# A Hyena/MLA encoder layer: the inverse DFT of its spectral stages as three products of f16 parts, three bins behind

## What is computed

```
def fft_conv(z, kf, bias):
    L = z.shape[1]
    zf32 = z.astype(jnp.float32)
    zf = jnp.fft.rfft(zf32, n=2 * L, axis=1)
    y = jnp.fft.irfft(zf * kf, n=2 * L, axis=1)[:, :L]
    return y + zf32 * bias.astype(jnp.float32)

def hyena_mixer(u, ...):
    v, x1, x2 = jnp.split(short_conv(u, conv_w, conv_b), 3, axis=-1)
    kf = hyena_filters(L, ...)                 # spectra of the implicit filters
    z = x1 * fft_conv(v, kf[:, 0], bias[0])
    z = x2 * fft_conv(z, kf[:, 1], bias[1])
```

## Time and profile before

| | us |
|---|---|
| median of 3 runs | 2887.83 (2886.19 to 2893.82) |
| the profiled execution | 2882.89 |
| its span in the profile | 2881.0 |

### The profile page before, as it was taken

One profiled execution on the slowest core, in us unless ns is written; L12 is line 12 of the kernel. 1 busy time (PEld: TensorE's weight loads), 2 busy tenths in 40 slices (PEclk: granted clock), 3 DMA queues, 4 the chain that ended last, 5 costly groups with the idle time before them and its releaser, 6 DMA issues. The chain is left out here.

```text
span 2881.0 us, 47562 instructions
## 1 busy us (share of the span) xinstructions
PE 2532.7 (88%) x17257; PEld 1429.3 (50%) x17257; DVE 2024.9 (70%) x2938; ACT 1772.1 (62%) x2980; POOL 1107.0 (38%) x1048
## 2 busy tenths in 40 slices
PE   6899999959999999988897896999910999999997
PEld 4455555525555555553332232455510666676664
DVE  5456555548888888878897896544367777777773
ACT  6644444329999999988555654433240777766761
POOL 1221212138888888877106600122120233333331
PEclk9999999959999999999999998999955999999998
DMA  7423323325311111107786787445341677776752
GB/s 183 125 59 92 92 80 90 98 64 181 106 24 24 38 38 38 38 16 251 270 302 221 276 302 261 135 151 165 110 166 34 203 234 224 226 221 211 221 150 57
DMA packets 269184, 416.04 MB, mean 144 GB/s; under 512 B 55646, under 2 KB 149214, under 8 KB 267424
## 3 DMA queue, kind: packets, MB, share of 16 engines
q1 hardware_dynamic: 219952, 344.39, 37.6%
q0 software_dynamic: 10752, 37.75, 5.4%
q10 hardware_dynamic: 38288, 31.37, 3.8%
HBM read 280.56 MB, written 132.86 MB: 143 GB/s over the span
## 5 line engine op out<-in xcount | busy, mean ns | idle before, releaser
L1162 POOL TENSOR_TENSOR at_p<-at_pf,at_p 128x512 f16<-128x512 f32 x424 | 510.6, 1214 | 138.0 <-ACT at_p L1296 110.7
L1424 DVE TENSOR_REDUCE at_mxs<-at_pM 128x1 f32<-128x512 f32 x512 | 342.4, 685 | 74.1 <-PE at_pM L1323 62.6
L1295 ACT ACTIVATE at_pf<-at_pS,at_scale 128x512 f32<-128x512 f32 x520 | 358.3, 689 | 30.1 <-PE at_pS L1348 29.2
L1296 ACT ACTIVATE at_p<-at_pS,at_scale 128x512 f16<-128x512 f32 x520 | 355.3, 683 | 0.0
L1367 PEld LDWEIGHTS at_pO<-at_vv,at_p 128*128 128x128 f16 x4160 | 233.8, 97 | 140.7 <-POOL at_p L1162 31.8
L1367 PE MATMUL at_pO<-at_vv,at_p 128*128 128x129 f16 x4160 | 267.8, 207 | 8.3 <-POOL at_p L1162 6.5
L1323 PE MATMUL at_pM<-at_k,at_q 96*128 96x512 f16 x512 | 190.2, 390 | 27.6 <-DVE at_q L1410 17.2
L1346 PE MATMUL at_pS<-at_q,at_k 97*128 97x512 f16 (+1 forms) x528 | 200.2, 379 | 3.9 <-issue 2.2
L1347 PE MATMUL at_pS<-at_q,at_k 96*128 96x512 f16 (+1 forms) x528 | 199.8, 378 | 0.0
L1348 PE MATMUL at_pS<-at_q,at_k 96*128 96x512 f16 (+1 forms) x528 | 198.6, 376 | 0.0
L2405 PE MATMUL mg_pU<-z,mg_yT 128*128 128x512 f16 x576 | 171.6, 380 | 2.8 <-DVE z L2493 2.1
(11 more groups left out here) (400 smaller groups left out, 6097.6 us busy)
## 6 DMA issues: line engine op xcount, KB each, us to landing
sp_rows<-s_F SPq DMA_DIRECT2D x76, 512.0 KB, 5.4
s_F<-fs_a SPq DMA_DIRECT2D x72, 512.0 KB, 3.0
mo_raw<-in_w_gate SPq DMA_DIRECT2D x32, 1024.0 KB
mo_raw<-in_w_up SPq DMA_DIRECT2D x32, 1024.0 KB, 6.9
mo_down<-in_w_down SPq DMA_DIRECT2D x32, 1024.0 KB, 4.9
s_G<-sp_gg SPq DMA_DIRECT2D x72, 256.0 KB, 4.1
sp_tab<-tab_spec SPq DMA_DIRECT2D x76, 224.0 KB, 3.9
s_QK<-pj_R ACTq DMA_DIRECT2D x18, 768.0 KB, 4.7
```

What stands on the lines that cost most here:

```text
L1162: eng.tensor_tensor(p2[r][:, :], pf[:, r, :], p1[r][:, :], ALU.subtract).then_inc(own_done if n in own else others_done, 1)
L1295: act.activation(pf[:, n % 4, :], pS[n % 2][:, 0:QB], ACT.Exp, scale=scale[:, 0:1])
L1296: act.activation(p1[n % 4][:, :], pS[n % 2][:, 0:QB], ACT.Exp, scale=scale[:, 0:1]).then_inc(pS_free, 1)
L1424: dve.tensor_reduce(mxs[:, j // NC, j % NC:j % NC + 1], pM[j % 2][:, :], AX.X, ALU.max).then_inc(pM_free, 1)
```

## The change

The inverse tables become pairs of f16 parts like the forward ones (same bytes). The product of the spectra, still made in f32 by VectorE, is split into an f16 high part by ScalarE (`split_pk`, after `move_x` of the next step) and an f16 low part by GpSimd, which subtracts the high part from the product. The inverse DFT is then six f16 products (high x high, low table x high, high table x low, two halves each) in place of two f32 ones, and it runs three steps behind instead of two. `pk` has two buffers (RING), its parts have four (LAG + 1); the output buffers become three, and a result is stored six steps behind instead of seven. The product is scaled down by 2^-18 so that it fits f16, which the last scale takes back.

```diff
--- before.py
+++ after.py
@@ -76,7 +76,7 @@
         back[b, :, P:] = np.concatenate([of_im, -of_re], 0)[:, order]
         spec[b, :, P:] = folded_spectrum(L, b)
     return (first.reshape(2, P, P).transpose(1, 0, 2), last.reshape(2, P, P).transpose(1, 0, 2),
-            np.concatenate([back.astype(np.float32), in_halves(spec)], -1))
+            np.concatenate([in_halves(back), in_halves(spec)], -1))
 
 
 TAB_SCALE = 2.0 ** 10
@@ -1887,8 +1887,10 @@
     N0 = NB[0] + 1
     STEPS = N0 + NB[1] + 1
     H = N2
-    PREP, LAG = 2, 2
-    ROWS, SPLIT, TABS, OUTS, STORE_LAG = 4, 3, 6, 4, 7
+    PREP, LAG = 2, 3
+    ROWS, SPLIT, TABS, OUTS, STORE_LAG = 4, 3, 6, 3, 6
+    RING, PK_SCALE = 2, 2.0 ** -18
+    assert 8 * MOST ** 2 * PK_SCALE <= MOST
     TW = P + N2
     with ExitStack() as ctx:
         def sb(name, shape, dt=F32):
@@ -1902,13 +1904,16 @@
 
         tab = [sb(f"tab{r}", [P, 2 * P + TW]) for r in range(TABS)]
         tabs = [t[:, 2 * P:].bitcast(F16) for t in tab]
+        backs = [t[:, 0:2 * P].bitcast(F16) for t in tab]
+        back_hi, back_lo = ([t[:, at:at + 2 * P] for t in backs] for at in (0, 2 * P))
         tab_hi, tab_lo = ([t[:, at:at + TW] for t in tabs] for at in (0, TW))
         cross = sb("cross", [P, P])
         cross_hi = cross[:, :].bitcast(F16)[:, 0:P]
         rows_in = [sb(f"rows{r}", [P, 2, DH]) for r in range(ROWS)]
         high, low = ([sb(f"{n}{r}", [P, 2, DH], F16) for r in range(SPLIT)] for n in ("high", "low"))
         xs = sb("xs", [P, 2, DH])
-        pk = [sb(f"pk{r}", [P, 2, DH]) for r in range(LAG + 1)]
+        pk = [sb(f"pk{r}", [P, 2, DH]) for r in range(RING)]
+        pk_hi, pk_lo = ([sb(f"pk_{n}{r}", [P, 2, DH], F16) for r in range(LAG + 1)] for n in ("hi", "lo"))
         gg, inverse = sb("gg", [P, OUTS, DH]), sb("inverse", [P, 2, DH])
         total, each, scale, back = sb("total", [P, 2]), sb("each", [P, NT + 4]), sb("scale", [P, 2]), sb("back", [P, 2])
         sized_by, mhalf = sb("sized_by", [P, 2]), sb("mhalf", [P, 1])
@@ -1923,6 +1928,7 @@
         cross_in, high_made, low_made = sem("cross_in"), sem("high_made"), sem("low_made")
         x_made, x_moved, k_made, multiplied = sem("x_made"), sem("x_moved"), sem("k_made"), sem("multiplied")
         g_made, g_moved, unscaled = sem("g_made"), sem("g_moved"), sem("unscaled")
+        pk_high, pk_low = sem("pk_high"), sem("pk_low")
         g_out = [sem(f"g_out{r}") for r in range(OUTS)]
         src, dst = ([stage_rows(io[x], g) for g in range(2)] for x in ("F", "G"))
         block = ctx.enter_context(nc.Block())
@@ -1970,9 +1976,19 @@
             pool.wait_ge(consts, 1)
             pool.wait_ge(floored, 1)
             pool.tensor_tensor(scale[:, 0:1], sized_by[:, 0:1], mhalf[:, :], ALU.pow).then_inc(rooted, 1)
+            for n in range(STEPS):
+                r = n % (LAG + 1)
+                pool.wait_ge(pk_high, n + 1)
+                pool.tensor_tensor(pk_lo[r][:, :, :], pk[n % RING][:, :, :], pk_hi[r][:, :, :], ALU.subtract).then_inc(pk_low, 1)
 
         @block.scalar
         def _(act):
+            def split_pk(n):
+                act.wait_ge(multiplied, n + 1)
+                if n > LAG:
+                    act.wait_ge(g_made, n - LAG)
+                act.activation(pk_hi[n % (LAG + 1)][:, :, :], pk[n % RING][:, :, :], ACT.Copy).then_inc(pk_high, 1)
+
             def prepare(n):
                 r = n % SPLIT
                 act.wait_ge(r_in[n % ROWS], 16 * (n // ROWS) + 16)
@@ -1989,7 +2005,8 @@
                 act.wait_ge(x_made, n + 1)
                 if n >= 2:
                     act.wait_ge(multiplied, n - 1)
-                act.activation(xs[:, n % 2, :], pX[n % 2][:, :], ACT.Copy, scale=TAB_SCALE ** -2).then_inc(x_moved, 1)
+                act.activation(xs[:, n % 2, :], pX[n % 2][:, :], ACT.Copy, scale=PK_SCALE * TAB_SCALE ** -2
+                               ).then_inc(x_moved, 1)
 
             act.wait_ge(summed, 1)
             act.activation(each[:, 0:NT], pSum[:, 0:NT], ACT.Copy, accum_out=total[:, 0:1]).then_inc(totalled, 1)
@@ -1998,8 +2015,11 @@
                 prepare(n)
             for n in range(STEPS):
                 move_x(n)
+                if n:
+                    split_pk(n - 1)
                 if n + PREP < STEPS:
                     prepare(n + PREP)
+            split_pk(STEPS - 1)
 
         @block.tensor
         def _(pe):
@@ -2035,10 +2055,12 @@
                 out, joins = pG[c % 2], n > 0 and opens(n - 1)
                 if not joins and c >= 2:
                     pe.wait_ge(g_moved, c - 1)
-                pe.wait_ge(multiplied, n + 1)
-                for m in range(2):
-                    last = pe.matmul(out[:, :], tab[t][:, m * P:(m + 1) * P], pk[n % (LAG + 1)][:, m, :],
-                                     start=(m == 0 and not joins), stop=(m == 1 and not opens(n)))
+                pe.wait_ge(pk_low, n + 1)
+                r = n % (LAG + 1)
+                pairs = [(w, x, m) for w, x in ((back_hi, pk_hi), (back_lo, pk_hi), (back_hi, pk_lo)) for m in range(2)]
+                for at, (w, x, m) in enumerate(pairs):
+                    last = pe.matmul(out[:, :], w[t][:, m * P:(m + 1) * P], x[r][:, m, :],
+                                     start=(at == 0 and not joins), stop=(at == 5 and not opens(n)))
                 last.then_inc(g_made, 1)
 
             pe.matmul(pSum, s["ones"][:, :], s["sizes"][:, :], start=True, stop=True).then_inc(summed, 1)
@@ -2063,9 +2085,9 @@
                 b = n % 2
                 dve.wait_ge(k_made, n + 1)
                 dve.wait_ge(x_moved, n + 1)
-                if n > LAG:
-                    dve.wait_ge(g_made, n - LAG)
-                dve.tensor_tensor(pk[n % (LAG + 1)][:, :, :], pK[b][:, :, :], xs[:, b, :].unsqueeze(1).to_broadcast([P, 2, DH]), ALU.mult
+                if n >= RING:
+                    dve.wait_ge(pk_low, n - RING + 1)
+                dve.tensor_tensor(pk[n % RING][:, :, :], pK[b][:, :, :], xs[:, b, :].unsqueeze(1).to_broadcast([P, 2, DH]), ALU.mult
                                   ).then_inc(multiplied, 1)
 
             def move(n):
@@ -2083,7 +2105,7 @@
             dve.wait_ge(floored, 2)
             dve.reciprocal(scale[:, 1:2], sized_by[:, 1:2]).then_inc(scaled, 1)
             dve.wait_ge(scaled, 1)
-            dve.tensor_scalar(back[:, 1:2], sized_by[:, 1:2], 1.0, None, ALU.mult).then_inc(backed, 1)
+            dve.tensor_scalar(back[:, 1:2], sized_by[:, 1:2], 1 / (PK_SCALE * TAB_SCALE), None, ALU.mult).then_inc(backed, 1)
             dve.wait_ge(rooted, 1)
             dve.reciprocal(back[:, 0:1], scale[:, 0:1]).then_inc(backed, 1)
             for n in range(PREP):
```

## The result

The changed kernel takes 2944.99 us (median of 4 runs, 2942.02 to 2948.15) against 2887.01 for the kernel before in the same comparison. The ratio is 1.0196, 95% interval 1.0181 to 1.0212: about 2% slower, by 58 us. The forecast was 2945, range 2905 to 2975.

What follows compares the result with a forecast made beforehand. TensorE was taken as the bound (3.24 us a step), VectorE only 0.17 behind. Loop 25.8, earlier steps 1.3 and tail 1.7 made 28.8 a stage, twice 57.6, on 2882.89: 2940.5, plus 4.9 to the median, 2945; range 2905 to 2975.

Steps and rivals of the forecast that it cites:

- The bound that goes: Inverse product on TensorE: six f16 products take 1.32 us for 1.81, TensorE 2.75 a step, no longer the bound.
- rival E: Both stages: the clock falls to the 1.2 GHz level in half of the steps, 53 us more, 2998; chance 0.08.
- High and low part: Split of the spectra's product: high part on ScalarE 1.14 us, low part on GpSimd 2.17 us a step.
- The loop through SyncE: SyncE's queue: the store waits for VectorE's move, the next rows load behind it; closes over two steps, 3.54 + landing.
- Its size: Step time in the SyncE loop: 4.10 us with the hold by GpSimd, 3.97 for the bare loop, against 3.24 before.
- L: Rows load from issue to landing, in SyncE's queue: taken as 4.4 us, with 3.9 and 5.5 as ends.
- The hold by GpSimd: VectorE's lows held by GpSimd's low part, 4.35 minus the step time, lifting the step from 3.97 to 4.10 us.
- Rival B: The SyncE loop without the hold: steps of 3.97 us, 47 us more in total, 2935; chance 0.07.
- The sum: Each stage: 25.8 us for the loop, 1.3 for steps ahead, 1.7 for the tail; 28.8, twice 57.6.
- Exclusion, 3.50 a step: VectorE's lows (1.33 us) and GpSimd's low part (2.17) exclude each other: at least 3.50 us a step.
- Rival C: Only the exclusion of lows and GpSimd binds, the loop is slack: 3.50 us a step, 22 more, 2910; chance 0.10.
- Rival D: Neither exclusion nor store hinders; VectorE becomes the bound at 3.07 us a step: -9 us, 2879; chance 0.07.

Runs made afterwards that it cites:

- the run with one column: Changed kernel, store six steps behind, GpSimd subtracting only the first of 512 columns in each half, the rest cleared: 2930.16 us, ratio 1.0154 against the kernel before.
- the run with the loop nearly open: Changed kernel with results stored seven steps behind instead of six: 2894.13 us against 2886.79 for the kernel before, ratio 1.0026.
- with one column and the store seven behind: Changed kernel, store seven steps behind, GpSimd subtracting only the first of 512 columns in each half: 2874.61 us, ratio 0.9957 against the kernel before.
- the half version two steps behind: Only the second half of the inverse product from f16 parts; inverse two, store seven steps behind as in the kernel before: 2874.76 us against 2890.20, ratio 0.9949.
- the doubled subtraction: Changed kernel with store seven steps behind and each GpSimd subtraction done twice: 3035.02 us in one run, against 2890.20 for the kernel before.

## Why the prediction was right, and where it was not

*The bound that goes.* Right. Six f16 products take 0.215 each, 1.29; TensorE is at 71% and its granted clock stays at 1.00 in both stages of the changed kernel, so rival E did not come; the last section has two runs where the clock did fall.

*High and low part.* The high part takes 1.04, not 1.14 (below the lower bound of 1.06, the f32 copy of the same size), the low part 2.13 (2.17).

*The loop through SyncE.* Right, and shown from both sides: opened in the changed kernel it gives back 51 us, closed in the kernel before it costs 47.

*Its size.* The period came out, 4.12 for 4.10, from two terms that were both off. L was put at 4.4 for a lighter DMA load; it stayed at 4.8 at a DMA share of 0.77, against 5.5 at 0.93. The other terms of the loop, put at 3.54, are 3.45 on average in the run with one column, so the bare loop is (3.45 + 4.75) / 2 = 4.10. The hold by GpSimd, which the forecast put on top with 0.13 a step (4.10 for 3.97), is 0.03 to 0.04. By the formula h = 4.35 - T it would be 0.2 for two steps at this T, and with ScalarE's faster high part 0.1 less; 0.05 and 0.09 were measured. Rival B, the loop without the hold, was nearer to the mechanism, with a larger L.

*The sum.* Per stage 28.8 us were forecast and 29.9 measured: 25.8 for the loop against 25.0, 1.3 for the steps ahead of it against 4.0 for the first seven, nothing for the last step against -0.8, and 1.7 for the tail against 1.7. L too short and the hold too long nearly cancel, and so do parts of the rest. That the median meets the forecast of 2945 is luck; that it lies in the upper part of the range is the loop.

*Exclusion, 3.50 a step.* This is the term that was furthest off. The runs show 3.21, already in the first steps of the changed kernel. I had added the lengths of the rows, 1.33 and 2.17, as if each engine shut the other out from its first to its last moment; about 0.17 us overlap at each change of turn (estimated above). A sign of it was in the rows: in rows 8 GpSimd's operation ends 1.14 after VectorE's, and alone it takes 1.21. In the sum it stood for 1.3 us a stage, and the first seven steps cost 4.0 all the same. There I had started from 3.24 a step. But in the kernel before steps 1 and 2, with no inverse product to make yet, take 2.45 and 2.63, and after the change 3.92 and 3.20, since low parts and lows now meet there; and the last of the seven, 4.69, is already in the loop. The last step gives 0.8 back. The tail is 1.7, as worked out.

*Rival C* took 3.50 for its price and so stood at 2910; the run with the loop nearly open gives 2894. *Rival D*, VectorE as the bound with -9 us, needs both hindrances gone. The run nearest to that, with one column and the store seven behind, gave -12, with late rows still in some of its steps. VectorE's own queue is 3.05 a step, not 3.07, and the half version two steps behind reaches it: 0.19 less than 3.24 in nearly every step.

*The Trainium skill's rule* on the shared port (SBUF — State Buffer, "Who interferes with whom") spoke against the change and was right in kind: the doubled subtraction shows the two taking turns. It says that the loser is blocked for the whole instruction; by the rows here it is the instruction but for about 0.17 us, 2.13 + 1.41 fit into 3.21.

*Left open.* Why L is 4.8 and not 4.4 with a store just ahead and the table behind wasn't separated into table and store. Nor does any run say why the rows land 0.24 us sooner in order 1 than in order 0 of the run with one column.

## What to carry to other kernels

In a queue that works in order, a store waits for the end of the pipeline and everything behind it in the queue waits too, so a change of how many steps the store lags, or of how late its result is made, must be followed to the loads behind it: count the steps between what the store waits for and what the next load feeds, and divide issue, landing and everything up to the next such result by that number. Compare it with the step for the longest landing, not only for the usual one: over three steps it was at the bound and single late rows still cost time, over four they didn't. When TensorE's work is moved to idle engines, first see how far the next engine is behind (0.17 us here) and move only as much as that; half of the move gave more than the whole.

## What the runs showed of the hardware

- GpSimd's 128x1024 subtraction and VectorE's operations with two SBUF inputs exclude each other except for about 0.17 us at each change of turn (estimated from 5.75 in 5.08 and 3.54 in 3.21). A low of 0.744 us took up to 2.1 in the first steps of the changed kernel; VectorE's operations with one PSUM input kept their 1.21 beside GpSimd (1444.62 with the store seven behind).
- The granted clock stayed at 1.00 in both stages of the changed kernel, with TensorE 71% busy in steps of 4.12 us. In steps of 5.08 us (the doubled subtraction) it was 1.00 from 1420 to 1460 us, with TensorE shown 59% and 58% busy, and 0.83 on average from 1460 to 1500, where the clock fell to the 1.2 GHz level at times and TensorE was shown 73% busy. In the run with one column it was 0.91 from 1440 to 1460 us, in steps of about 4.1.
- The landing time of a 512 KB load fell with the DMA share, but slowly: 5.7 us at 0.97, 5.5 at 0.93, 4.8 at 0.77, and 4.2 at 0.60 (medians of order 0 in the half version two steps behind, the kernel before, the changed kernel and the doubled subtraction).
